# Differential attention in a two-block transformer kernel: value pieces tile by tile, outputs between them, norm weight at the transposes

## The reference, cut to what matters

```python
q, k, v = jnp.split(h @ w_in, 3, axis=-1)
...
s = jnp.einsum('bhiqd,bhikd->bhiqk', qb, k[:, :, :, :L]).astype(f32)
p = jax.nn.softmax(jnp.where(mask, s, -jnp.inf), axis=-1)
a = p[:, :, 0] - lam * p[:, :, 1]
outs.append(jnp.einsum('bhqk,bhkv->bhqv', a.astype(v.dtype), v[:, :, :L]))
...
o = rmsnorm(o, subln_g) * (1.0 - lambda_init)
...
return o @ w_o
```

## Time and profile before

| what | value |
|---|---|
| median of 3 runs | 1386.47 us (1384.35 to 1387.46) |
| profiled execution, device time | 1384.33 us |
| its span in the trace | 1382.5 us |
| PE busy | 1343.6 us, 97% of the span |
| DVE, ACT, POOL busy | 952.2, 668.8, 82.2 us |

### The profile page before, as it was taken

The page is one execution under the profiler, slowest core; times in us unless marked ns, Lnnn a source line. Parts: engine busy times, 40 slices in busy tenths (PEclk is TensorE's granted clock), DMA queues, the critical chain, the costliest instruction groups (busy, mean ns, idle before and its releaser), DMA issues.

```text
span 1382.5 us, 19853 instructions
## 1 busy us (share of the span) xinstructions
PE 1343.6 (97%) x8344; PEld 1184.8 (86%) x8344; DVE 952.2 (69%) x1110; ACT 668.8 (48%) x876; POOL 82.2 (6%) x149
## 2 busy tenths in 40 slices
PE   6999999999998999999999999999999999999997
PEld 2897898998886799998898778999998977999996
DVE  4998787776897777655784444887777445787774
ACT  3733554433646564444634443654445455654442
POOL 0212111110111100000000000000000000000000
PEclk9999999999999999999999999999999999999999
DMA  9995498786590466555355434455453632365530
GB/s 376 362 362 179 152 339 302 292 293 226 207 357 31 185 227 244 213 185 197 137 213 185 165 129 161 154 212 183 183 185 143 223 121 91 123 226 190 190 127 31
DMA packets 46680, 279.92 MB, mean 202 GB/s; under 512 B 5264, under 2 KB 5648, under 8 KB 19584
## 3 DMA queue, kind: packets, MB, share of 16 engines
q1 hardware_dynamic: 33696, 231.57, 45.6%
q0 software_dynamic: 12896, 47.09, 9.0%
HBM read 277.59 MB, written 1.05 MB: 202 GB/s over the span
## 4 chain that ended last, share of the span: by engine, by line
PE 91%; DVE 4%; ACT 1%; DMA 1%; issue 1%; SPq 1%; POOL 0%; POOLq 0%; DVEq 0%; ACTq 0%
PE ps L1705 33%; PE ps L1869 12%; PE ps L1870 12%; PE ps L1871 12%; PE ps L1766 6%; PE ps L1805 5%; PE ps L2098 1%; PE ps L1836 1%; DMA early_a<-in_ada_w 1%; DVE w_lo L1030 1%; PE ps L1788 1%; PE ps L1904 1%; PE ps L2314 1%; PE ps L2215 0%; PE ps L1912 0%
## 5 line engine op out<-in xcount | busy, mean ns | idle before, releaser
L1030 DVE TENSOR_TENSOR w_lo<-raw,w_hi 128x2048 fp32r<-128x2048 f32 x209 | 477.2, 2289 | 163.2 <-ACT w_hi L631 162.4
L631 ACT ACTIVATE w_hi<-raw 128x2048 fp32r<-128x2048 f32 x209 | 398.7, 1912 | 192.6 <-PE ps L1705 137.9
L1869 PE MATMUL ps<-h_hi,w_hi 128*128 128x256 f32 x1344 | 382.1, 284 | 0.0
L1871 PE MATMUL ps<-h_hi,w_lo 128*128 128x256 f32 x1344 | 380.5, 283 | 0.0
L1870 PE MATMUL ps<-h_lo,w_hi 128*128 128x256 f32 x1344 | 380.5, 283 | 0.0
L1870 PEld LDWEIGHTS ps<-h_lo,w_hi 128*128 128x128 f32 x1344 | 256.5, 191 | 2.1 <-issue 0.5
L1869 PEld LDWEIGHTS ps<-h_hi,w_hi 128*128 128x128 f32 x1344 | 256.5, 191 | 2.0 <-issue 0.5
L1871 PEld LDWEIGHTS ps<-h_hi,w_lo 128*128 128x128 f32 x1344 | 256.5, 191 | 0.0
L1599 DVE SCALAR_TENSOR_TENSOR f_cv<-ps,cols,f_cv 128x254 f32<-128x254 f32 (+1 forms) x176 | 76.7, 477 | 73.0 <-ACT f_cv L942 71.4
L1705 PE MATMUL ps<-w_hi,hid_lo 128*128 128x512 f32 x344 | 106.9, 392 | 0.0
L1705 PE MATMUL ps<-w_lo,hid_hi 128*128 128x512 f32 x344 | 106.7, 391 | 0.0
(11 more groups left out here) (320 smaller groups left out, 1785.8 us busy)
## 6 DMA issues: line engine op xcount, KB each, us to landing
raw<-in_stream SPq DMA_DIRECT2D x209, 1024.0 KB, 4.8
ada<-in_ada_w POOLq DMA_DIRECT2D x80, 512.0 KB, 6.0
ada<-in_ada_w SPq DMA_DIRECT2D x4, 512.0 KB, 5.6
early_hi<-in_ada_w SPq DMA_DIRECT2D x4, 512.0 KB, 12.4
early_lo<-in_ada_w SPq DMA_DIRECT2D x4, 512.0 KB, 12.4
row<-in_gate_b POOLq DMA_DIRECT2D x4, 512.0 KB, 5.0
x<-in_x SPq DMA_DIRECT2D x1, 1024.0 KB, 8.6
early_a<-in_ada_w SPq DMA_DIRECT2D x2, 512.0 KB, 15.8
```

The costliest lines, as they stand in the source:

```text
L631: act.activation(w_hi[:, s, :], raw[:, s, :], ACT.Copy).then_inc(hi_done[s], 1)
L1030: dve.tensor_tensor(w_lo[:, s, :], raw[:, s, :], w_hi[:, s, :].bitcast(f32), ALU.subtract)\
L1869: pe.matmul(out, wh, h_hi[:, kt, :], start=kt == 0, stop=False)
L1871: last = pe.matmul(out, wl, h_hi[:, kt, :], start=False, stop=kt == KT - 1)
```

## The change

It has five parts, all in this stage.

1. The second half of the value projection runs tile by tile: pieces 8 to 11 are tile 0 (bank 0), 12 to 15 tile 1 (bank 1). Slots are freed by pieces 12 to 15.
2. Outputs get places of their own (`d_place`): heads 0 and 1 in bank 1, 2 and 3 in bank 0, then banks 1, 7, 3, 5. They stand in PE's list between the value pieces, and no output waits for an earlier one's reading. Piece 12 waits for heads 0 and 1 to be scaled.
3. Map 1 is no longer divided. `d_combine` multiplies lambda, the second reciprocal and the first sum (one small instruction) and adds the maps; the reciprocals are kept in `d_rn`. The first reciprocal comes in as scale of ACT's square, and as a third POOL instruction in the norm factor.
4. ACT, not DVE, scales the outputs: `d_square` (scale from `d_rn`), then `d_scaled`, which reads PSUM again and writes `d_o`; the copy is gone. DVE's `d_scale` is gone.
5. The norm weight is a column `subc` (128x1 instead of 128x128) applied when the transposed banks are split (`d_split` on ACT, `d_rest` on DVE). The banks of the transposes are 6, 4, 7, 5, and pair 0 is turned before head 7.

ACT's and DVE's lists are rewritten to fit; `hi(C_DV + 5)` moves behind the scaling of head 6, `lo(C_DV + 4)` from head 2 to head 6.

```diff
+        def d_place(h):
+            return ((1, 0), (1, T), (0, 0), (0, T), (1, 0), (7, 0), (3, 0), (5, 0))[h]
+        def do_bank(b):
+            return (6, 4, 7, 5)[b]
...
-                inverse_rms(stat[:, 1, 2 * h:2 * h + 2], stat[:, 0, 2 * h:2 * h + 2], 2, DDV).then_inc(drs, 1)
+                out = stat[:, 1, 2 * h:2 * h + 2]
+                pc.inc(inverse_rms(out, stat[:, 0, 2 * h:2 * h + 2], 2, DDV))
+                pool.wait_ge(pool_chain, pc.n)
+                pool.tensor_tensor(out, out, d_rn[:, h, 0:2], ALU.mult).then_inc(drs, 1)
...
-            def d_out(h):
-                act.wait_ge(do_mm, h + 1)
-                out = ps[:, h % 2, 0:T].rearrange("p (t k) -> p t k", t=TT)
+            def d_square(h):
+                act.wait_ge(do_mm, h + 2 if h in (0, 2) else h + 1)
+                b, first = d_place(h)
                 for t in range(TT):
-                    act.activation(h_lo[:, 2 * (h % 2) + t, 0:DDV], out[:, t, :], ACT.Square,
-                                   accum_out=stat[:, 0, 2 * h + t:2 * h + t + 1])
-                act.activation(d_o[:, :, h * DDV:(h + 1) * DDV], out, ACT.Copy).then_inc(do_act, 1)
+                    last = act.activation(d_o[:, t, h * DDV:(h + 1) * DDV], ps[:, b, first + t * P:first + (t + 1) * P],
+                                          ACT.Square, scale=d_rn[:, h, t:t + 1],
+                                          accum_out=stat[:, 0, 2 * h + t:2 * h + t + 1])
+                last.then_inc(do_act, 1)
+            def d_scaled(h):
+                act.wait_ge(drs, h + 1)
+                b, first = d_place(h)
+                for t in range(TT):
+                    last = act.activation(d_o[:, t, h * DDV:(h + 1) * DDV], ps[:, b, first + t * P:first + (t + 1) * P],
+                                          ACT.Identity, scale=stat[:, 1, 2 * h + t:2 * h + t + 1])
+                last.then_inc(o_done, 1)
+            def d_split(b):
+                act.wait_ge(tr_done, 4 * TR_DO + b + 1)
+                act.activation(h_hi[:, 2 * b:2 * b + 2, :].rearrange("p k t -> p (k t)"), ps[:, do_bank(b), :],
+                               ACT.Identity, scale=subc[:, 0:1]).then_inc(hh_done, 1)
...
-                link(dve.reciprocal(d_st[:, r, 2, :], d_st[:, r, 1, :]))
-                dve.tensor_scalar(d_st[:, r, 2, 2:4], d_st[:, r, 2, 2:4], lamc[:, 0:1], None, ALU.mult)
-                parts = ((1, 0, 2 * P), (0, 2 * P, P))
-                for t, a, n in parts:
-                    last = dve.tensor_scalar(d_p[:, r, 0, a:a + n], d_p[:, r, 0, a:a + n],
-                                             d_st[:, r, 2, t:t + 1], None, ALU.mult)
-                link(last)
+                link(dve.reciprocal(d_rn[:, h, :], d_st[:, r, 1, :]))
+                link(dve.scalar_tensor_tensor(d_st[:, r, 2, 2:4], d_rn[:, h, 2:4], lamc[:, 0:1], d_st[:, r, 1, 0:2],
+                                              ALU.mult, ALU.mult))
...
-            def d_scale(h):
...
+            def d_rest(b):
+                dve.wait_ge(hh_done, HL_BASE[TR_DO] + b + 1)
+                dve.scalar_tensor_tensor(h_lo[:, 2 * b:2 * b + 2, :].rearrange("p k t -> p (k t)"), ps[:, do_bank(b), :],
+                                         subc[:, 0:1],
...
             def d_output(h):
                 pe.wait_ge(dat_done, h + 1)
-                if h >= 2:
-                    pe.wait_ge(do_act, h - 1)
+                if h in (0, 2, 4):
+                    pe.wait_ge(*y_read(Y_DV, 1 + h // 2))
...
+            d_transposes_out(range(1))
             d_turn(7)
...
+            for h in range(4, 7):
+                d_output(h)
+            pe.wait_ge(dat_done, 8)
+            d_transposes_out(range(1, 2))
             d_output(7)
...
-            h_rows(C_DO, 0, 4, lambda b: (do_act, DH_), fresh=TR_DO)
+            h_rows(C_DO, 0, 4, lambda b: (o_done, GH_ + (4, 5, 5, 7)[b]), fresh=TR_DO)
+            d_transposes_out(range(2, 4))
```

More of the change, by code:

```diff
@@ L576, in _ @@
             norm(1)
[L577 removed]
+            for dst, src in ((lamv[:, :], lam_d), (subc[:, :], sub_d[0:1, :].rearrange("o d -> d o"))):
                 pool.dma_start(dst, src).then_inc(lam_in, 16)
@@ L843, in _, with d_values @@
             d_features(d_kt, 4)
-            def d_values(n):
-                half = slice(n * 512, (n + 1) * 512)
-                for t in range(TT):
-                    act.wait_ge(*y_written(Y_DV, 2 * n + t))
-                    act.activation(d_v[:, t, half], ps[:, t, :], ACT.Copy).then_inc(y_act, 1)
+            def d_values(n, t):
+                act.wait_ge(*y_written(Y_DV, 2 * n + t))
+                act.activation(d_v[:, t, n * 512:(n + 1) * 512], ps[:, t, :], ACT.Copy).then_inc(y_act, 1)
             def d_exp(h):
@@ L872, in _ @@
             d_exp(0)
             d_exp(1)
-            d_values(0)
+            d_values(0, 0)
+            d_values(0, 1)
             d_exp(2)
             d_exp(3)
-            hi(C_DV + 4)
-            d_exp(4)
-            d_exp(5)
-            hi(C_DV + 5)
-            d_exp(6)
-            d_values(1)
-            d_out(0)
-            d_exp(7)
-            for h in range(1, DH_):
-                d_out(h)
-            split_stage(TR_DO, h_hi, range(3))
+            d_square(0)
+            d_square(1)
@@ new lines, in _ @@
+            d_exp(4)
+            d_scaled(0)
+            d_scaled(1)
+            d_exp(5)
+            d_values(1, 0)
+            d_exp(6)
+            hi(C_DV + 4)
+            d_exp(7)
+            d_square(2)
+            d_square(3)
+            d_values(1, 1)
+            d_scaled(2)
+            d_scaled(3)
+            d_split(0)
+            d_square(4)
+            d_square(5)
+            d_square(6)
+            d_scaled(4)
+            d_split(1)
+            d_scaled(5)
+            d_square(7)
@@ L888, in _ @@
+            d_scaled(6)
+            hi(C_DV + 5)
+            d_scaled(7)
             hi(C_DV + 6)
+            d_split(2)
             hi(C_DV + 7)
-            split_stage(TR_DO, h_hi, range(3, 4))
+            d_split(3)
             hi(C_M1)
@@ L1472, in _ @@
                     d_maxima(h + 3)
-                if h == 2:
+                if h == 6:
                     lo(C_DV + 4)
-                if h >= 5:
-                    d_scale(2 * h - 10)
-                    d_scale(2 * h - 9)
-            d_scale(DH_ - 2)
-            d_scale(DH_ - 1)
-            split_stage(TR_DO, h_lo, h_hi, range(3))
+            dve.wait_ge(sub_done, 1)
+            d_rest(0)
+            d_rest(1)
             lo(C_DV + 5)
+            d_rest(2)
             lo(C_DV + 6)
-            split_stage(TR_DO, h_lo, h_hi, range(3, 4))
+            d_rest(3)
             lo(C_DV + 7)
@@ L1879, in transposes @@
                         pe.wait_ge(hl_done, HL_BASE[TR_RA] + b + 1)
+                    bank = do_bank(b) if stage == TR_DO else 4 + b
                     for j in range(2):
@@ L2091, in d_value_piece @@
                     pe.wait_ge(*(y_read(Y_DV, t) if n else y_read(Y_DK, t)))
+                    if n and t:
+                        pe.wait_ge(o_done, GH_ + 2)
                 s = (C_DV + i) % NSLOT if n or t else chunk_ready(C_DV + i)
@@ L2155, in _ @@
             d_turn(0)
+            d_value_pieces(8, 1)
             d_scores(3)
[L2157 to L2166 removed]
+            d_turn(1)
+            d_value_pieces(9, 1)
             d_output(0)
             d_output(1)
[L2169 removed]
+            d_scores(4)
+            d_turn(2)
+            d_value_pieces(10, 1)
+            d_scores(5)
+            d_turn(3)
+            d_value_pieces(11, 1)
+            d_scores(6)
+            d_value_pieces(12, 1)
+            d_turn(4)
+            d_value_pieces(13, 1)
+            d_scores(7)
             d_output(2)
             d_output(3)
+            d_turn(5)
+            d_value_pieces(14, 1)
             d_turn(6)
[L2173 to L2174 removed]
+            d_value_pieces(15, 1)
+            d_transposes_out = lambda pairs: transposes(TR_DO, d_o, lambda b: (o_done, GH_ + 2 * b + 2), pairs)
+            d_transposes_out(range(1))
             d_turn(7)
[L2176 removed]
+            for h in range(4, 7):
+                d_output(h)
+            pe.wait_ge(dat_done, 8)
+            d_transposes_out(range(1, 2))
             d_output(7)
[L2178 to L2180 removed]
+            h_rows(C_DO, 0, 4, lambda b: (o_done, GH_ + (4, 5, 5, 7)[b]), fresh=TR_DO)
+            d_transposes_out(range(2, 4))
             last_three(range(C_DO + 1, C_DO + 4), h_pair(1), lambda i: (hl_done, HL_BASE[TR_DO] + i + 2),
```

43 lines of the change are left out of this document (14 added, 29 removed).

## The result

The changed kernel took **1389.34 us** (median of 20 runs, 1386.62 to 1394.54), the kernel before beside it on the same chip 1386.4 (20 runs, 1383.43 to 1391.04): ratio 1.0021, 95% interval 1.0012 to 1.0029. Slower by 2.9 us, where 4.4 faster was forecast. The profiled execution took 1389.04 with a span of 1387.3, against 1384.33 and 1382.5.

What follows compares the result with a forecast made beforehand. PE, carrying 91% of the chain, was taken as the bound. Waits of 8.4 us go and 4.1 come: 4.3 by waits, 4.5 by the clock, 4.4 taken, so 1386.47 becomes 1382.1 us; range 1380.0 to 1385.2.

Steps and rivals of the forecast that it cites:

- What costs nothing: Behind the gate matmuls: program the same and hangs on PE; weight loads, column load and slot 0 cost no time.
- slower: Rival: GpSimd in series with ACT ends the stage, PE loses 2.4 us, 1388.9; chance 0.05 (slower by over 0.2%: 0.03).
- Waits that go: PE, first scores to gate matmuls: seven waits, 7.9 us from start to start, plus 0.5 of smaller gaps, some 8.4.
- The new waits: PE in the new order: 0.6 + 0.2 + 0.4 + 0.8 + 1.3 + 0.8 = 4.1 us.
- Turns: PE at the turned weights of heads 6 and 7: waits of 0.6 and 0.2 us, turn 6 for its combine.
- Outputs 0 and 1: PE's outputs of heads 0 and 1, placed between value pieces: stand at 421.8 to 423.2 us.
- Copy 7: After turn 7: the copy stands behind weight rest lo(C_DV + 4) on DVE, so PE waits 0.4 us.
- Banks 1 and 3: Output projection: PE waits 0.8 and 1.3 us for banks freed by heads 4 and 6; the second starts at 448.0.
- Weights: Last three projection chunks: the second finds its weights at 456.2, 0.8 us late.
- GpSimd's third instruction: Norm factor on GpSimd: the added 128x2 product takes 0.3 us, making 1.36 per head.
- stretched by VectorE: Rival: GpSimd instructions stretch beside DVE's weight rest, one or two at 0.73 extra; gain 3.4, 1383.1; chance 0.10.
- ACT's lengths: ACT in the stage: two scalings take 0.58 us, a split 0.60, a head's squares 0.70.

Runs made afterwards that it cites:

- e1: Changed kernel with 352 bytes of filler ahead of the arena, so every arena tile lies where it lay before; 1383.49 us, ratio 0.9975.
- e6: Changed kernel, arena back in place, without the third GpSimd instruction (first softmax sum left out of the norm factor); 1381.34 us, ratio 0.9963.
- e5: Changed kernel, arena back in place, weight rest lo(C_DV + 4) moved on VectorE behind the copy of head 7's turned weights; 1382.53 us, ratio 0.9967.

## Why the prediction was wrong

**The step that failed** is the first sentence of "What costs nothing": "Behind the gate matmuls the program is the same and hangs on PE." Its instructions are the same and it does hang on PE, and just so each ns on one of 1176 row products goes straight to the end. The addresses are not the same. I costed instructions, waits and loads, and passed over the line of the diff that swaps a 512-byte tile for one of 32 and one of 128. It isn't only what stands behind the stage, either: 1.7 us are lost ahead of it, between 154 and 386 us, where the prediction has no term at all. No rival had it. The rival "slower" gives 1388.9, near the 1389.34 measured, but by GpSimd in series, which took 2.16 of a stage that still gained; that nearness is luck. The addresses cost 5.5 us by the trace, 6.4 by the medians, against a stage gain of 3.05 to 3.4: the sign is this alone, since e1 with the same instructions is faster than before.

**The stage: mechanism right, size off.** Forecast 4.4, measured 3.05.
- *Waits that go*: all seven went, scores have none. I priced each at 0.16 more than its idle time and added 0.5 for small gaps, 8.4; by the windows view PE's idle time was 6.96 in all. So the side of the gains was 1.4 too large. The new waits, 4.1 forecast, were 3.75 by the same view, although they hold the stretch that I had not put among them.
- *Turns*: forecast 0.6 for turn 6 and 0.2 for turn 7; measured 0.38 and none. Outputs 0 and 1 begin 11.2 behind the first scores, forecast 11.1. The layout by hand held up to here.
- *Copy 7*: forecast 0.4, measured 0.37 at the pair of transposes ahead of head 7's output. By the profile it was ACT's scaling of head 3 that held them, which ends at 447.07, 0.25 behind the copy. Right size, another cause: with e6, without the third instruction, this wait is gone though the rest still stands ahead of the copy.
- *Banks 1 and 3*: forecast 0.8 and 1.3, measured 1.33 and 0.99. The second product to wait began 39.0 behind the first scores, forecast 37.3. Most of these 1.7 us are ACT's wait of 1.48 for GpSimd, handed on: e5, without it, has this product 38.0 behind the first scores, its own wait of 0.32 included.
- *Weights*: forecast 0.8, measured 0.62.
- *GpSimd's third instruction*: forecast 0.3 with its gap a chain of 1.36 per head; measured 0.20, and 1.33 from head to head (442.04 to 443.37). But once 1.89. The rival "stretched by VectorE" named the mechanism, named `lo(C_DV + 4)`, and gave 3.4 for the stage, which is the nearest of all cases. Its price was too low: I took the one long case of the earlier trace rows, 0.92, as what a stretched instruction takes. That one had begun 1.42 us into its rest; the price that all the caught ones show is what was left of the rest. By that an instruction of 0.2 could take up to the 2.29 of the whole. I gave this 0.10 because "most factors are made where DVE idles": head 3's was not, and one is enough.
- *ACT's lengths*, from start to start: a square 0.35, a pair of scalings 0.51, a split 0.57 (446.44 to 446.95 to 447.52), against 0.35, 0.58 and 0.60. ACT was no slower than thought; it was kept waiting.

With the stretch away (e5) the stage gains 4.14, within 0.3 of the forecast; with the arena back in place too, the whole is at 1382.5, where 1382.1 was forecast for the change. The range ended at 1385.2, and "slower" had 0.03. Even without the stretch the changed kernel would have been at about 1388.

## What to carry to other kernels

When a change alters the size of any tile, list which tiles behind it move, and whether a matmul operand is among them: compare the mean ns of the untouched matmul groups before looking at waits. A rise in PE's busy time at an equal count is a sign, once the granted clock of the two profiles is the same. Where row products (512 moving columns) dominate, try the distance between moving and stationary tiles as a parameter, with a few unused floats. And a small GpSimd instruction on a chain must not start while VectorE runs a long one on two SBUF operands: price it at the rest of that instruction.
